# Sliding attention in a two-model block: two output banks, projections emptied behind the exponentials, the queries' low part made half a period later

## The reference

```python
q = (h @ w_q).reshape(B, S, SW_KV_HEADS, SW_GROUP, HEAD_DIM)     # 4 groups x 4 heads x 64
q = apply_rope(rms_norm(q, q_norm), cos, sin)
s = jnp.einsum('bnqhgd,bnkhd->bnhgqk', qb, kw) * (1.0 / math.sqrt(HEAD_DIM))
s = jnp.where(valid, s, NEG_INF)                 # each query sees its own and the previous block of 128
m = jnp.maximum(jnp.max(s, axis=-1, keepdims=True), sink)
e = jnp.exp(s - m)
p = e / (jnp.sum(e, axis=-1, keepdims=True) + jnp.exp(sink - m))
o = jnp.einsum('bnhgqk,bnkhd->bnqhgd', p, vw)
return o.reshape(B, S, SW_HEADS * HEAD_DIM) @ w_o
```

## Time and profile before

| what | value |
|---|---|
| three runs | 2948.87, 2948.88, 2951.93 us (median 2948.88) |
| the profiled execution | 2948.14 us, span 2946.3 us |
| PE busy over the span | 2805.5 us (95%) |
| DVE, ACT, POOL busy | 1795.1 (61%), 1110.2 (38%), 155.7 us (5%) |
| first sliding `q` stage | 755.0 to 937.2 us |
| second sliding `q` stage | 2281 to 2508 us |

### The profile page before, as it was taken

One profiled execution on the slowest core, in us unless ns is written; L12 is line 12 of the kernel. 1 busy time (PEld: TensorE's weight loads), 2 busy tenths in 40 slices (PEclk: granted clock), 3 DMA queues, 4 the chain that ended last, 5 costly groups with the idle time before them and its releaser, 6 DMA issues.

```text
span 2946.3 us, 41568 instructions
## 1 busy us (share of the span) xinstructions
PE 2805.5 (95%) x14475; PEld 2333.3 (79%) x14475; DVE 1795.1 (61%) x2841; ACT 1110.2 (38%) x1809; POOL 155.7 (5%) x195
## 2 busy tenths in 40 slices
PE   7989999999887999999998999999999998999998
PEld 6777688887776788887886888888888887788886
DVE  6767577675764577676895554353456554564645
ACT  5444332323564322223332332232223666352422
POOL 4111000000110000000110000000000000000000
PEclk8999999999998999999997999999999999999999
DMA  3111245452101355442561121121111000232222
GB/s 113 65 57 44 86 169 195 157 174 105 44 30 37 115 178 185 165 163 68 138 148 43 44 69 65 54 71 64 52 51 56 15 30 15 72 103 90 93 92 66
DMA packets 73491, 263.73 MB, mean 90 GB/s; under 512 B 8304, under 2 KB 10608, under 8 KB 70768
## 3 DMA queue, kind: packets, MB, share of 16 engines
q1 hardware_dynamic: 69152, 249.99, 24.8%
q0 software_dynamic: 4176, 11.63, 2.2%
HBM read 247.87 MB, written 2.10 MB: 85 GB/s over the span
## 4 chain that ended last, share of the span: by engine, by line
PE 61%; issue 16%; DVE 13%; ACT 4%; DVEq 2%; DMA 2%; POOLq 1%; POOL 0%; ACTq 0%; SPq 0%
PE psum L1921 17%; PE psum L1923 16%; PE psum L1922 16%; DMA sw_vb<-tap_prod 2%; PE psum L2320 2%; DVE work L1440 1%; ACT work L1070 1%; DVE w_lo L1268 1%; PE psum L2072 1%; ACT sw_pt L1082 1%; DVE work L1558 1%; PE psum L2050 1%; PE psum L2309 1%; DVE tok_ms L1568 1%; PE psum L2051 1%
## 5 line engine op out<-in xcount | busy, mean ns | idle before, releaser
L1921 PE MATMUL psum<-hx_hi,w_hi 128*128 128x512 f32 x1568 | 625.9, 399 | 4.7 <-DVE hc_lo L1549 1.7
L1923 PE MATMUL psum<-hx_hi,w_lo 128*128 128x512 f32 x1568 | 620.8, 396 | 0.0
L1922 PE MATMUL psum<-hx_lo,w_hi 128*128 128x512 f32 x1568 | 616.0, 393 | 0.0
L731 ACT ACTIVATE w_hi<-w_raw 128x1024 fp32r<-128x1024 f32 (+1 forms) x328 | 344.6, 1051 | 510.5 <-PE psum L1923 203.3
L1268 DVE TENSOR_TENSOR w_lo<-w_raw,w_hi 128x1024 fp32r<-128x1024 f32 (+1 forms) x328 | 398.3, 1214 | 185.6 <-ACT w_hi L731 167.7
L1923 PEld LDWEIGHTS psum<-hx_hi,w_lo 128*128 128x128 f32 x1568 | 294.3, 188 | 74.4
L1921 PEld LDWEIGHTS psum<-hx_hi,w_hi 128*128 128x128 f32 x1568 | 293.9, 187 | 61.3 <-issue 5.4
L1922 PEld LDWEIGHTS psum<-hx_lo,w_hi 128*128 128x128 f32 x1568 | 294.4, 188 | 47.8
L1921 PE MATMUL psum<-a_hi,w_hi 128*128 128x512 f32 (+1 forms) x656 | 234.0, 357 | 9.2 <-DVE a_lo L1380 8.9
L1923 PE MATMUL psum<-a_hi,w_lo 128*128 128x512 f32 (+1 forms) x656 | 234.5, 357 | 0.0
L1922 PE MATMUL psum<-a_lo,w_hi 128*128 128x512 f32 (+1 forms) x656 | 233.3, 356 | 0.0
(11 more groups left out here) (307 smaller groups left out, 4957.4 us busy)
## 6 DMA issues: line engine op xcount, KB each, us to landing
mod_w<-in_w_mod SPq DMA_DIRECT2D x96, 512.0 KB, 3.8
w_raw<-in_fup SPq DMA_DIRECT2D x88, 512.0 KB, 4.6
w_raw<-in_cup SPq DMA_DIRECT2D x88, 512.0 KB, 3.6
w_raw<-in_fdown SPq DMA_DIRECT2D x32, 512.0 KB, 4.7
w_raw<-in_cdown SPq DMA_DIRECT2D x32, 512.0 KB, 3.7
sw_vb<-tap_prod POOLq DMA_DIRECT2D x29, 391.5 KB, 5.4
w_raw<-in_da_qkv SPq DMA_DIRECT2D x6, 1536.0 KB, 6.3
w_raw<-in_fdown SPq DMA_DIRECT2D x16, 384.0 KB, 3.0
```

What stands on the lines that cost most here:

```text
L731: r = act.activation(w_hi[:, off:off + n], w_raw[:, raw:raw + n], ACT.Copy)
L1921: pe.matmul(dst, wh, xh, start=first, stop=False)
L1922: pe.matmul(dst, wh, xl, start=False, stop=False)
L1923: return pe.matmul(dst, wl, xh, start=False, stop=last)
```

## The change

In the first sliding stage only:

- The scores use three banks (1 to 3) in turn instead of four, and the outputs of m go into bank 4 + m % 2, with the spread inverses beside them. `values` waits for the outputs of two m before, not of one; `scores` may start once the exponentials of three halves before are done, where it was four.
- On ACT, `evac_proj(m + 2)` in the even half is replaced by `evac_proj(m + 3)` in the odd half, behind the sinks and ahead of `turned`; `evac_proj(2)` stands ahead of the loop.
- On DVE, `q_low(m + 2)` at the end of the odd half is replaced by `q_low(m + 1)` in the even half, between the maxima and `rotated`.

In both sliding stages a refill comes in quarters: on ACT in the four halves of m = 2 and 3 (6 and 7), on DVE each one half later.

The diff, cut to its core (the second stage's refills change alike, with 512 columns in place of 1024; `spread_out`, `outputs` and `spread_inverse` take `out_bank(st, m)` where they had bank 5):

```diff
@@ span and the bank of the outputs
-            a = 512 * (1 + p % 4) + n * x
+            a = 512 * (1 + p % 3) + n * x
             return a, a + n
+
+        def out_bank(st, m):
+
+            return 5 if st["ctx"] else 4 + m % 2
@@ ACT, refill of the weights' high parts
                     if st.get("wgain"):
-                        for k in range(4 * part, 4 * part + 4):
+                        for k in range(2 * part, 2 * part + 2):
...
-                    r.then_inc(s_hi if part else S["whi"], 1)
+                    r.then_inc(s_hi if part == 3 else S["whi"], 1)
@@ ACT, the loop
                 turned(1)
+                if not st["ctx"]:
+                    evac_proj(2)
                 for p in range(34):
                     m, half = p // 2, p % 2
                     parts = len(chunks(st, p - 1)) if 0 < p < 33 else 0
-                    if half == 0 and m < 14:
+                    if half == 0 and m < 14 and st["ctx"]:
                         evac_proj(m + 2)
...
                     if half and m < 16:
                         sinks(m)
+                    if half and m < 13 and not st["ctx"]:
+                        evac_proj(m + 3)
                     if half and m < 14:
                         turned(m + 2)
                     if half and m:
                         outs(m - 1)
-                    if m in (2, 6):
-                        refill(m // 4 + 2, half)
+                    if m in (2, 3, 6, 7):
+                        refill(m // 4 + 2, p % 4)
@@ DVE, refill of the low parts
-                    if part == 0:
-                        dve.wait_ge(S["whi"], b - 1)
+                    if part < 3:
+                        dve.wait_ge(S["whi"], 3 * (b - 2) + part + 1)
...
@@ DVE, the loop
                         outputs(m - 1)
+                    if half == 0 and 0 < m < 15 and not st["ctx"]:
+                        q_low(m + 1)
                     if half == 0 and m < 14:
                         rotated(m + 2)
                         doubled(m + 2)
                     if half and m < 16:
                         sink_args(m)
-                    if half and m < 14:
+                    if half and m < 14 and st["ctx"]:
                         q_low(m + 2)
-                    if m in (2, 6) and half:
-                        refill(m // 4 + 2, 0)
-                    if m in (3, 7) and half == 0:
-                        refill(m // 4 + 2, 1)
+                    if (p - 1) // 2 in (2, 3, 6, 7):
+                        refill((p - 1) // 8 + 2, (p - 1) % 4)
@@ PE, scores
-                        if p >= 4:
-                            pe.wait_ge(S["ex"], p - 3)
+                        if p >= 3:
+                            pe.wait_ge(S["ex"], p - 2)
@@ PE, values
-                    if p % 2 == 0 and c == 0 and m:
-                        pe.wait_ge(S["osb"], m)
+                    shared = 1 if st["ctx"] else 2
+                    if p % 2 == 0 and c == 0 and m >= shared:
+                        pe.wait_ge(S["osb"], m + 1 - shared)
                     for i, k in enumerate(chunks(st, p)[c]):
-                        r = pe.matmul(pb[:, 5, 0:256], v_cols(tiles[k], g, p % 2), sw_pt[:, n % 2, 256 * i:256 * i + 256],
+                        r = pe.matmul(pb[:, out_bank(st, m), 0:256], v_cols(tiles[k], g, p % 2), sw_pt[:, n % 2, 256 * i:256 * i + 256],
```

More of the change, by code:

```diff
@@ L1094, in spread_out @@
                         act.wait_ge(S["osb"], m)
-                    act.activation(sw_invb[:], pb[:, 5, 256:512], ACT.Copy).then_inc(S["invb"], 1)
+                    act.activation(sw_invb[:], pb[:, out_bank(st, m), 256:512], ACT.Copy).then_inc(S["invb"], 1)
                     act.drain()
@@ L1115, in refill @@
                     else:
-                        r = act.activation(w_hi[:, off + D * part:off + D * (part + 1)],
-                                           w_raw[:, raw + D * part:raw + D * (part + 1)], ACT.Copy)
-                    r.then_inc(s_hi if part else S["whi"], 1)
+                        r = act.activation(w_hi[:, off + 512 * part:off + 512 * (part + 1)],
+                                           w_raw[:, raw + 512 * part:raw + 512 * (part + 1)], ACT.Copy)
+                    r.then_inc(s_hi if part == 3 else S["whi"], 1)
                     act.drain()
@@ L1839, in outputs @@
                     dve.wait_ge(S["invb"], m + 1)
-                    dve.tensor_tensor(sw_osb[:], pb[:, 5, 0:256], sw_invb[:], ALU.mult).then_inc(S["osb"], 1)
+                    dve.tensor_tensor(sw_osb[:], pb[:, out_bank(st, m), 0:256], sw_invb[:], ALU.mult).then_inc(S["osb"], 1)
                     dve.drain()
@@ L1853, in refill @@
                     n, raw, off, idx = slot_of(st, b)
-                    if part == 0:
-                        dve.wait_ge(S["whi"], b - 1)
+                    if part < 3:
+                        dve.wait_ge(S["whi"], 3 * (b - 2) + part + 1)
                     else:
                         dve.wait_ge(s_hi, st["block0"] + b + 1)
-                    cols = slice(off + D * part, off + D * (part + 1))
+                    cols = slice(off + 512 * part, off + 512 * (part + 1))
                     if st.get("wgain"):
-                        for k in range(4 * part, 4 * part + 4):
+                        for k in range(2 * part, 2 * part + 2):
                             r = low_weights(st, off, raw, k)
                     else:
-                        r = dve.tensor_tensor(w_lo[:, cols], w_raw[:, raw + D * part:raw + D * (part + 1)],
+                        r = dve.tensor_tensor(w_lo[:, cols], w_raw[:, raw + 512 * part:raw + 512 * (part + 1)],
                                               w_hi[:, cols].bitcast(F32), ALU.subtract)
-                    if part:
+                    if part == 3:
                         r.then_inc(s_lo, 1)
@@ L2326, in spread_inverse @@
                     for a in range(2):
-                        r = pe.matmul(pb[:, 5, 256 + a * P:256 + (a + 1) * P],
+                        r = pe.matmul(pb[:, out_bank(st, m), 256 + a * P:256 + (a + 1) * P],
                                       inv_wide[:, 2 * a:2 * a + 2, :].rearrange("p a f -> p (a f)"), ident[:],
```

## The result

The changed kernel takes 2952.7 us (median of 20 runs, 2950.79 to 2961.54), the kernel before 2949.32 us (20 runs, 2943.71 to 2952.6). The medians differ by 3.4 us (0.11%). The ratio, which goes by the means (4.7 us apart), is 1.0016 with a 95% interval of 1.001 to 1.0023: slower by 0.16%, clear of 1 and inside the 0.2% that the prediction counted as the same, though the upper end of the interval is not. Sixteen of the changed kernel's runs lie from 2950.8 to 2954.4 us and four from 2956.9 to 2961.5, and the four pull its mean above its median. The prediction was 2955.9 us, with 2949 to 2968 as its range. The profiled execution took 2951.27 us with a span of 2949.5.

A forecast was written before the change was run, and what follows sets the result against it. The prediction took the first sliding stage to be a loop of waits between DVE and ACT, with PE off the chain. Its terms, 10.8 - 5.0 - 1.5 + 0 + 2.7 = +7.0 us, gave 2955.9 us, range 2949 to 2968.

The forecast's parts named there:

- Term 1: First sliding stage's loop: DVE's wait moves to `outs`, `q_low` joins the chain; +0.90 us per period, twelve times, +10.8 us.
- Term 2: Weight refills in the first sliding stage: quarters cost 3.8 us where halves cost 8.8, net -5.0 us.
- Term 5: TensorE clock in the first sliding stage: longer periods bring two more low-clock stretches, +2.7 us (0 to +20).
- second rival: First sliding stage: the clock falls in nearly every period, +18 in place of 2.7, 2971.2 us; chance 0.16.
- Term 3: End of the first sliding stage: a second output bank lets the last transposes start earlier, -1.5 us (0 to -3).
- Term 4: Second sliding stage, which gets only the quarters: 0 us, with -2 and +1.5 as the ends.
- The first: First sliding stage: the clock stays as it is and adds no cost, 2953.2 us; chance 0.31.
- The third: First sliding stage: the output bank was the limit; -12.5 us, no loop or clock cost, 2936.4 us; chance 0.03.

The follow-up runs named there:

- The eight combinations: Runs with `evac_proj` moved or not, `q_low` moved or not, and one or two output banks; ordinary periods from 9.30 to 11.06 us.
- the kernel with the added matmuls: Changed kernel with matmuls of zeros filling PE's idle time at two places of a period: 2958.79 us, against 2954.08 without.

## Why the prediction was right, and where it was off

**Term 1, the loop: right.** Predicted +0.90 per period (0.87 to 1.04), twelve times; measured 10.28 - 9.41 = 0.87, twelve times +10.4. The removed wait came back one instruction later, at the low part of the outputs, and `outs` released it. The allowance of 0.03 for a late projection was not needed: `evac_proj` starts 0.13 behind the sinks. (The upper end of 1.04 does not follow from its terms, 0.87 and the whole 0.14 give 1.01.) The eight combinations give the same 0.87 as 0.98 for the move of `evac_proj` less 0.11 for that of `q_low`.

**Term 2, the refills: near in size, wrong in cause.** Predicted -5.0; the six periods around the two refills grew by 0.44 and 0.66 us where 6 x 0.87 = 5.22 would have been due: -4.1. Two periods around the first take 815.33 - 793.49 = 21.84 us, where the prediction said some 22.5. The failed step is the saving put down to the quarters, 8.8 us for the halves against 3.8 for the second and fourth quarter "between doubling and odd maxima". That is where they stand, but in the changed kernel whole halves cost as little, 2.1 us a refill for 2.2. What shrank is what the longer wait for `outs` covers, which the prediction had named only in passing (1.64 us "and longer now").

**Term 5, the clock: too high, and put down to the wrong idle time.** Predicted +2.7 for two more falls. The loop had two more, at 805, 826, 860 and 874 us, where before there were two, at 805 and 846. Beside the kernel with the added matmuls, whose clock does not fall there and whose ordinary periods are the same, the falls at 805 and 860 cost 0.3 us each (11.56 for 11.23, and 32.28 for 31.99 in three periods), that at 826 nothing (10.28 for 10.28), and that at 874 cost 1.5 (12.14 for 10.59). What the two falls before had cost no run shows. In the difference between the two kernels I can read 1.2 us in the period of the last one: it is 1.86 over an ordinary one, where before it was 0.65 over (10.06). The rest of the loop's +6.89 is -0.6 us: -0.3 in the period between the refills (9.71 before, 10.28 now), the other half at the start and the end. The step that failed in cause is "the longer period adds 0.9 us of idle PE time to each m" as what brings the falls: ordinary periods have that idle time and no fall, as the second rival below shows.

**Term 3, the end: right direction, -3.0 for -1.5,** and how much of it is the bank is open. The low clock behind the last maxima lasted from 928 to 941 before and from 935 to 942 now. With one bank in the changed kernel, last maxima to residual sum take 23.1 us as in the kernel before (23.0), with two 20.1; with two in the kernel before, at a low clock from 933 to 943, 22.2. The other pairs give 0.9 (23.0 and 22.0, `evac_proj` in its old place and `q_low` moved) and 1.3 (19.7 and 18.4, the other way round). The bank's own part is between 0.8 and 3.0, and I cannot separate it from the clock.

**Term 4, the second stage: +1.2 for 0,** within its ends. With halves in the changed kernel it was 0.0, but 0.9 with halves and `outs` first. Over all profiles it is 1.0 to 2.3 with quarters and -0.1 to 2.3 with halves, so the quarters are not shown as the cause.

**The sum.** For the profiled pair, in us:

| | predicted | measured |
|---|---|---|
| up to the stage's first maxima | 0 | +0.75 |
| loop, twelve periods | +10.8 | +10.4 |
| refills | -5.0 | -4.1 |
| clock in the loop | +2.7 | +1.2 |
| single other periods | 0 | -0.6 |
| end of the stage | -1.5 | -3.0 |
| unchanged stretch behind it | 0 | -2.7 |
| second sliding stage | 0 | +1.2 |
| together | +7.0 | +3.1 |

The stage cost 4.7 us in the first profile and 4.9 in the second. The -2.7 come from a stage that the prediction did not look at, since no line of it changes. Without them the profiled difference would be 5.9 us, the very 0.2% at which the prediction drew its line, so that the time came out as the same is in part luck. The prediction itself had given slower and the same 0.46 each.

**The rivals.** The first (clock as before, 2953.2) comes closest in time to the median, by luck: the clock did cost something in the loop, and the -2.7 of the unchanged stretch hide it. The third was priced without term 2, which the second bank would not have undone; with it the sum would have been 2931.4. The second (a fall in nearly every period) did not occur: four falls in the loop in the first profile and three in the second. The Trainium skill, "TensorE: Matmul & The Clock Gate", section "A second HAM failure mode: psum-queue depth-cycling", would have made it the forecast. This trace does not bear that out. In ordinary periods PE idles twice, 0.92 to 0.94 us and 1.01 to 1.03 us in one piece, and the clock stays up. Of the four falls three come within 1.5 us behind a single piece of 1.7 to 1.9 us, two of them in the refills' periods, where PE waits that long for `sw_pt`. The fourth, at 826, comes behind two shorter pieces, 0.91 and 0.66 us. Yet two more pieces of 1.9 us, at 816.55 and 847.62, bring no fall, so the length of one piece does not decide it alone. Before, both falls in the loop came with single pieces of 2.6 and 2.7 us (waits for `sw_sq` in the refills' periods). The rows of the changed kernel, first pieces of idle time, then windows, the last one of an ordinary period:

```profile
816.55 1.13 PE L2329 MATMUL psum<-sw_pt,sw_va 128*128 128x256 f32 x4 [1.93 <-ACT sw_pt L1086]
858.84 1.13 PE L2329 MATMUL psum<-sw_pt,sw_va 128*128 128x256 f32 x4 [1.93 <-ACT sw_pt L1086]
873.38 0.66 PE L2263 MATMUL psum<-ident,sw_dup 128*128 128x128 f32 x4 [1.71 <-DVE sw_dup L1790]
891.04 1.13 PE L2329 MATMUL psum<-sw_pt,sw_vb 128*128 128x256 f32 x4 [0.93 <-ACT sw_pt L1086]
```

```profile
822.20:825.60 3.40, 2.09 (x14) 1.49 (x12) 0.79 (x4) 2.82 (x9) 0.40 (x1) 1.00 0.00 0
825.60:829.00 3.40, 3.15 (x14) 2.97 (x14) 2.73 (x8) 1.53 (x6) 0.30 (x1) 0.58 0.00 0
870.30:873.70 3.40, 1.63 (x12) 1.17 (x11) 2.81 (x7) 1.64 (x4) 1.01 (x1) 1.00 0.01 2
873.70:877.10 3.40, 3.40 (x16) 3.04 (x14) 1.67 (x7) 1.52 (x5) 0.14 (x1) 0.54 0.03 7
892.71:896.11 3.40, 2.38 (x21) 2.11 (x20) 2.81 (x7) 1.64 (x4) 1.01 (x1) 1.00 0.00 0
```

## What to carry to other kernels

When an in-order engine waits for one piece of another's work, list the next pieces it needs from that engine and their place in the other's order: taking the first wait away only uncovers the next. Here the gain lay in the place of one statement, the piece that is waited for put directly behind its trigger, and everything that nobody waits for behind that. It took 1.46 us off the period of the changed kernel (10.28 to 8.82) and 0.48 where `evac_proj` stood in its old place (9.30 to 8.82). The three versions with it are 8 to 19 us faster than the kernel before, where the change as made lost 3. `outs` first in the kernel before, with no other edit, was not run.

In the loop a second buffer is worth what its wait costs on the chain that the other edits leave: 0 us per period without the early `evac_proj`, 0.68 us per period with it.

## What was not expected of the hardware

Time moves in stages that no edit touches. From the first residual sum behind the first sliding stage to that of the feed-forward stage (the third and fourth mark of the table) it is 651.4 us in the kernel before, 648.7 and 648.9 in two profiles of the changed kernel, 651.2 with its refills in halves, 646.8 with the move of `evac_proj` alone and 652.3 with `evac_proj` late and `outs` first. These 5.5 us are more than the whole effect of the change. The differences arise in the feed-forward stage and go with longer or shorter stretches at a low clock there, but why they differ between kernels is open. The changed kernel's own runs go from 2949.98 to 2959.99 us on one chip.

Idle time of PE that no chain holds went with a lower clock: with `evac_proj` late and `outs` first, all ordinary periods were 8.82 us as with `evac_proj` early, and the kernel was 10 us slower. This is one pair of kernels. The added matmuls kept the clock at its full level from 785 to 915 us, and it was low for 13.5 us instead of 6.5 directly after them.
